# A decoder layer on one core: array quarters in the RWKV products, five last transfers, rows gathered unscaled

## The reference, cut to what matters

```python
def step(state, inp):
    r_t, w_t, k_t, v_t, kk_t, a_t = inp
    sa = jnp.einsum('bhvk,bhk->bhv', state, -kk_t)
    state = (state * w_t[:, :, None, :] + sa[..., None] * (kk_t * a_t)[:, :, None, :]
             + v_t[..., None] * k_t[:, :, None, :])
    return state, jnp.einsum('bhvk,bhk->bhv', state, r_t)
```

```python
h = rms_norm(x, norm_ffn[l])
...
for e in range(N_EXPERTS):
    hid = jax.nn.silu(h @ w_gate[e]) * (h @ w_up[e])
    y = y + combine[..., e:e + 1] * (hid @ w_down[e])
...
return rms_norm(x, norm_final)
```

## Time and profile before

| what | value |
|---|---|
| median of 3 runs | 647.74 us (647.39 to 648.77) |
| the profiled execution | 647.7 us, its span 645.8 us |
| granted PE clock over the span | 0.979 |
| PE busy | 596.3 us (92%) |
| DVE / ACT / POOL busy | 218.3 / 139.2 / 20.6 us |
| DMA | 158.94 MB, mean 246 GB/s |

### The profile page before, as it was taken

One profiled execution on the slowest core, in us unless ns is written; L12 is line 12 of the kernel. 1 busy time (PEld: TensorE's weight loads), 2 busy tenths in 40 slices (PEclk: granted clock), 3 DMA queues, 4 the chain that ended last, 5 costly groups with the idle time before them and its releaser, 6 DMA issues.

```text
span 645.8 us, 11725 instructions
## 1 busy us (share of the span) xinstructions
PE 596.3 (92%) x4936; PEld 434.2 (67%) x4936; DVE 218.3 (34%) x598; ACT 139.2 (22%) x353; POOL 20.6 (3%) x24
## 2 busy tenths in 40 slices
PE   8999999999999999999999999998989988757793
PEld 8988887878877877777788888894434442313241
DVE  3152448625334566356400222234121121102022
ACT  3110233052243353444411000001110111000013
POOL 1000000001100103001000000000000000000000
PEclk9999999999999999999999999999999999969697
DMA  8584344731301111101339993888999999999993
GB/s 320 195 323 176 127 145 160 303 131 66 123 16 62 67 67 67 67 4 66 130 123 420 420 397 137 361 356 312 420 421 421 421 420 420 422 421 421 421 389 108
DMA packets 27287, 158.94 MB, mean 246 GB/s; under 512 B 2896, under 2 KB 7136, under 8 KB 9440
## 3 DMA queue, kind: packets, MB, share of 16 engines
q1 hardware_dynamic: 24224, 137.71, 54.4%
q10 hardware_dynamic: 3008, 20.45, 7.6%
HBM read 157.07 MB, written 1.07 MB: 245 GB/s over the span
## 4 chain that ended last, share of the span: by engine, by line
PE 62%; issue 32%; DVE 3%; ACT 1%; DMA 1%; POOL 0%; POOLq 0%; DVEq 0%; ACTq 0%; SPq 0%
PE bank L615 44%; PE bank L841 3%; PE bank L944 2%; PE bank L647 2%; PE bank L973 2%; PE bank L993 2%; PE bank L630 1%; DMA ring<-front 1%; PE bank L957 1%; ACT tok L1590 1%; PE bank L878 1%; PE bank L897 1%; DVE work L1789 1%; PE bank L908 1%; PE bank L1059 0%
## 5 line engine op out<-in xcount | busy, mean ns | idle before, releaser
L615 PE MATMUL bank<-hT,ring 128*128 128x256 f32 x864 | 199.6, 383 | 0.3 <-ACTq L1433 0.3
L615 PEld LDWEIGHTS bank<-hT,ring 128*128 128x128 f32 x864 | 159.6, 190 | 30.4 <-issue 10.4
L615 PE MATMUL bank<-yT,ring 128*128 128x256 f32 x256 | 55.4, 379 | 0.0
L615 PEld LDWEIGHTS bank<-yT,ring 128*128 128x128 f32 x256 | 48.6, 190 | 6.6
L1421 ACT ACTIVATE work<-bank 128x512 f32<-128x512 f32 (+2 forms) x44 | 22.6, 514 | 107.8 <-PE bank L1240 48.9
L1286 PE MATMUL bank<-ring,work 128*32 128x512 f32 (+1 forms) x192 | 34.7, 649 | 10.6 <-DMA yT<-experts 7.2
L1789 DVE TENSOR_TENSOR work<-bank,table 128x512 f32<-128x512 f32 (+1 forms) x22 | 11.6, 544 | 95.0 <-PE bank L1233 88.3
L1233 PEld LDWEIGHTS bank<-work,tok 128*128 128x128 f32 x256 | 30.2, 192 | 10.0 <-issue 10.0
L1590 ACT ACTIVATE tok<-tok,small 128x128 f32<-128x128 f32 (+1 forms) x64 | 28.4, 445 | 23.0 <-DVE small L2017 21.4
L1233 PE MATMUL bank<-work,tok 128*128 128x128 f32 x256 | 31.5, 278 | 0.8 <-DVE work L1793 0.8
L1224 PE MATMUL bank<-ring,work 128*32 128x512 f32 x240 | 29.6, 597 | 2.9 <-DMA ring<-experts 2.8
(11 more groups left out here) (255 smaller groups left out, 728.4 us busy)
## 6 DMA issues: line engine op xcount, KB each, us to landing
ring<-front SPq DMA_DIRECT2D x47, 1024.0 KB, 4.9
ring<-experts SPq DMA_DIRECT2D x40, 1024.0 KB, 24.6
work<-experts SPq DMA_DIRECT2D x9, 1024.0 KB, 27.7
ring<-experts ACTq DMA_DIRECT2D x8, 1024.0 KB, 13.8
table<-experts SPq DMA_DIRECT2D x6, 1024.0 KB, 27.2
yT<-experts SPq DMA_DIRECT2D x6, 1024.0 KB, 26.8
hT<-experts SPq DMA_DIRECT2D x4, 1024.0 KB, 24.3
work<-experts ACTq DMA_DIRECT2D x3, 1024.0 KB, 28.0
```

The source lines that it names most:

```text
L615: return first(pe.matmul(o, l, r, start=(k == 0), stop=(k == n - 1)))
```

## The change

Four edits.

1. *RWKV products.* For heads of odd `p` (in `solve`: for the second bank) the output's partition half is swapped (`half = c ^ p`), and the loops alternate between the banks, so that neighbours use different quarters. The swap is undone by the copies: DVE's copy of `y{i}1` and ACT's of `xu{i}1` become two copies of 64 partitions each.
2. *Router and seats.* A small table, two memsets and the slot numbers are made ahead of the wait for x. The counting matrix has -1024 on its diagonal, so that a count below zero means membership; `seat` compares the counts in PSUM with shifted slot numbers and writes `sel` itself. `scale_seats` is gone.
3. *Unscaled rows.* The gathered rows lack 1/rms. In each gang PE makes `half_root` for each slot (two matmuls with one column), ACT copies it to SBUF, and it is the scale of the tanh; the square of 1/rms goes into the combine weights. The turned weights of gang 0 come ahead of its last gate and up product.
4. *Last transfers and end.* The last gang's down chunks come in five parts (`PIECES`: each of the two row halves of columns 0 to 511, both halves of 512 to 767, each half of 768 to 1023), 20 transfers. PE works through them as they land. The root is taken by ACT (Sqrt, one token tile after the other) and DVE's reciprocal instead of POOL; DVE copies the second and third part.

```diff
-    put("earlier", (r[:, None] < r[None, :]) * 1.0)
+    put("earlier", (r[:, None] < r[None, :]) * 1.0 - np.eye(P) * OUTSIDE)
...
-                    for n in range(2):
-                        o = begin(f"xu{i}{n}")
-                        for h in range(4):
+                    xbank = [begin(f"xu{i}{n}") for n in range(2)]
+                    for h in range(4):
+                        for n in range(2):
                             for c in range(2):
                                 rows = slice(64 - 64 * c, 128 - 64 * c)
-                                last = pe.matmul(o[64 * c:64 * c + 64, h * P:(h + 1) * P], zinv[rows, 4 * n + h, :],
+                                half = c ^ n
+                                last = pe.matmul(xbank[n][64 * half:64 * half + 64, h * P:(h + 1) * P], zinv[rows, 4 * n + h, :],
                                                  rhs[rows, 4 * n + h, :, :], start=True, stop=True)
...
-                    for p in range(2):
-                        rows = slice(64 * p, 64 * p + 64)
-                        yb = bank[plan[f"y{i}{p}"][0]]
-                        for m in range(4):
-                            last = pe.matmul(yb[64 * c:64 * c + 64, m * DH:(m + 1) * DH],
+                    for m in range(4):
+                        for p in range(2):
+                            rows = slice(64 * p, 64 * p + 64)
+                            last = pe.matmul(y_rows(i, p, c)[:, m * DH:(m + 1) * DH],
                                              ar[rows, m, i, 1, 64 * c:64 * c + 64], state[rows, (2 * i + c) % 2, m, :],
                                              start=False, stop=True, skip_group_check=True)
...
+                    for m in range(4):
+                        for product in range(2):
+                            for p in range(2):
+                                h = 2 * m + p
+                                for c in range(2):
+                                    rows = slice(64 * c, 64 * c + 64)
+                                    right = vrow[rows, h * DH:(h + 1) * DH] if product else rhs[rows, h, 1, :]
+                                    last = pe.matmul(y_rows(i, p, c)[:, m * DH:(m + 1) * DH],
+                                                     amat[rows, h, 1 + 2 * product, :], right,
+                                                     start=(m == product == 0), stop=False, skip_group_check=True)
...
+            def y_rows(i, p, c):
+                half = c ^ p
+                return bank[plan[f"y{i}{p}"][0]][64 * half:64 * half + 64, :]
...
                     for i in range(NT):
+                        pe.matmul(bank[5][:, 0:1], sel[:, i, :], half_root[:, i:i + 1], start=(i == 0), stop=(i == 1))
...
+                        down_part(bank[0], *LAST[0], fs=(0,))
+                        pe.wait_ge(q["late_loaded1"], 16 * GANG)
+                        down_part(bank[0], *LAST[0], fs=(1,))
+                        scatter_last(0, 0)
...
-            pool.wait_ge(q["last_in"], 1)
-            pool.tensor_tensor(stat[:, 8:8 + NT], stat[:, 0:NT], cn("neghalf")[:, 0:NT], ALU.pow).then_inc(q["last_root"], 1)
...
+                            for c in range(2):
+                                ins = copy(rhs[64 * c:64 * c + 64, 4:8, :, :], solved[64 - 64 * c:128 - 64 * c])
...
+            def root(i):
+                act.wait_ge(q["squared"], 2 * NT + i + 1)
+                act.wait_ge(q["last_total"], 1)
+                act.activation(stat[:, i:i + 1], stat[:, 26 + 4 * i:27 + 4 * i], ACT.Sqrt, bias=stat[:, 18 + i:19 + i])\
...
-                    act.activation(gtanh, bank[4][:, 0:DE], ACT.Tanh, scale=0.5).then_inc(q["gtanh_ready"], 1)
+                    act.wait_ge(q["slot_root"], gang + 1)
+                    act.activation(gtanh, bank[4][:, 0:DE], ACT.Tanh, scale=slot_root).then_inc(q["gtanh_ready"], 1)
...
+                    if p == 0:
+                        chain(dve.tensor_copy(yv[:, :, p, :], yb))
+                    else:
+                        for c in range(2):
+                            chain(dve.tensor_copy(yv[64 * c:64 * c + 64, :, p, :], yb[64 - 64 * c:128 - 64 * c]), hold=(c == 1))
...
-            chain(stt(place[:, :, 0:E], b0[:, 0:2 * E].rearrange("p (i e) -> p i e", i=2), 1.0, member, ALU.add, ALU.mult))
...
-                    ts(sel[:, i, :], wsel[:, i, :], stat[:, 8 + i:9 + i], None, ALU.mult).then_inc(q["sel_ready"], 1)
...
+                    o = sel[:, i, :].rearrange("p (e s) -> p e s", e=GANG)
+                    tt(o, like(places[:, i, gang * GANG:(gang + 1) * GANG][:, :, None], [P, GANG, CAP]), slots,
+                       ALU.is_equal).then_inc(q["sel_ready"], 1)
```

More of the change, by code:

```diff
@@ L311, in build_layer @@
         halves = small[:, 192:224]
+        seats = halves
+        half_root, half_square, slot_root = stat[:, 40:42], stat[:, 42:44], stat[:, 44:45]
         rtf = work[:, 8 * S + 2 * E:LOW]
@@ L1281, in gathered_experts, with down_part @@
                     pe.wait_ge(q["ghidT_ready"], gang + 1)
-                    def down_part(n, o, lo, w, release):
-                        for f in range(2):
+                    def down_part(o, lo, w, fs=(0, 1), release=False):
+                        for f in fs:
                             for e in range(GANG):
@@ L1698, in finish @@
                 act.dma_start(out[(NT - 1) * P:NT * P, :], res[:, NT - 1, :]).then_inc(q["stored"], 16)
+            SQUARES = [(n, i) for n in range(len(LAST)) for i in range(NT)]
             def sum_squares(n, i):
@@ L1747, in dense_experts @@
                 second_weight()
-                act.wait_ge(q["root_ready"], 2 * NT + 1)
-                act.wait_ge(q["residual_held"], 2 * NT)
-                for i in range(NT):
-                    copy(tok[:, i, :], tok[:, i, :], scale=stat[:, 8 + i:9 + i]).then_inc(q["xn2_ready"], 1)
                 act.wait_ge(q["wsel_ready"], 1)
@@ L2191, in _ @@
                         chain(tt(merged[:, 2 * n:2 * n + 2, :], macc, mtmp, ALU.add), "merged_ready")
+            fall = cn("falling")
+            pair = [P, EPG, EPG]
+            least = scratch[:, 512:576].rearrange("p (e f) -> p e f", e=EPG)
+            chain(tt(least, like(fall[:, None, 0:EPG], pair), like(fall[:, 0:EPG, None], pair), ALU.is_lt))
+            chain(ts(least, least, 1.2e-38, None, ALU.mult), hold=False)
+            chain(dve.memset(small[:, 112:112 + 2 * (E + GANG)], 0.0), hold=False)
+            chain(ts(seats, fall[:, 0:CAP], -(OUTSIDE + 1.0), None, ALU.add))
             dve.wait_ge(q["x_again"], 16)
@@ L2292, in weigh_seats @@
                     w = wsel[:, i, :].rearrange("p (e s) -> p e s", e=GANG)
-                    ins = tt(w, w, like(combine[:, i, gang * GANG:(gang + 1) * GANG][:, :, None], [P, GANG, CAP]), ALU.mult)
+                    chosen = sel[:, i, :].rearrange("p (e s) -> p e s", e=GANG)
+                    ins = tt(w, chosen, like(combine[:, i, gang * GANG:(gang + 1) * GANG][:, :, None], [P, GANG, CAP]), ALU.mult)
                     if i == 1:
                         ins.then_inc(q["wsel_ready"], 1)
-            seat(0)
-            scale_seats(0)
+            seat(0, counted)
+            chain(dve.tensor_copy(place[:, :, 0:E], counted))
+            dve.sem_inc(bank_free[plan["places"][0]], 1)
+            root = stat[:, 8:8 + NT]
+            chain(ts(half_root, root, 0.5, None, ALU.mult), hold=False)
+            chain(stt(half_square, root, 0.5, root, ALU.mult, ALU.mult), hold=False)
             chain(dve.tensor_reduce(rt("m2"), rt("h2"), AXX, ALU.add))
@@ L2403, in dense_experts @@
                 diagonal_gains()
-                front_gain()
+                for i in range(NT):
+                    front_gain(i)
                 finish()
```

196 lines of the change are left out of this document (85 added, 111 removed).

## The result

The changed kernel takes 643.18 us (median of five runs, 642.21 to 645.20), the kernel before 647.74 (five runs, 647.11 to 648.77). The ratio is 0.9922, 95% interval 0.9906 to 0.9937. Forecast were 642.0 us, within 640.9 to 644.6. The profiled execution of the changed kernel took 642.21 us (span 640.3, and 1.9 around it).

A forecast was written before the change was run, and what follows sets the result against it. PE was taken to bound the first stage, expert transfers the second, a dependent chain the tail. From 647.7 us, less 3.95 (RWKV), 0.2 (gather) and 1.6 (tail), plus 0.1 (transfers), gave 642.0 us, range 640.9 to 644.6.

The forecast's parts named there:

- RWKV: Stage one, where PE sets the time: solve, local y and state y blocks shorten, less 0.4 for copies; 3.95 us gained.
- The waits ahead of the yT turn: Sign: PE's waits between the last y block and the last yT turn grow together by about 0.7 us.
- Rivals 1: RWKV gain is eaten: softmax copies on ACT or longer copies make PE wait; half of 3.95 goes, 644.0 us; chance 0.15.
- rival 5: RWKV y blocks: row halves writing one bank take turns, so they stay as they are; 1.64 us lost, 643.6; chance 0.05.
- rival 2: Front shortens, tail doesn't: last landing or a lagging DMA engine sets the end; 643.7 us; chance 0.13.
- First gather: Router to first gather: DVE ready some 0.8 us sooner, but PE's branch limits the gain; 0.2 us taken.
- Transfers: Expert transfers: same bytes in 20 issues instead of 12; eight more completions in a full queue cost 0.1 us.
- Rival 4: Transfers: issues bind, four more at 1.8 us each are 7.2 us, 649.2 us; chance 0.05.
- Tail: After the last landing: PE's products and scatters end 1.0 us earlier, the root saves 0.55 to 0.65; together 1.6 us.
- The root: End of the tail: ACT root and reciprocal replace POOL's pow, with tile 0 scaled during tile 1's squares; gain 0.55 to 0.65 us.
- Rival 3: Tail: more, shorter waits lower the granted clock from 1.0 to half; +3 us, 645.0 us; chance 0.07.
- The stores: End of the tail: the stores behind the last scaling stay as they are, a change of 0.

The follow-up runs named there:

- y_two_quarters: Changed kernel with both y banks laid out as before, so local y uses two of four quarters, and one copy for each bank: 644.41 us.
- thirtysix_issues: Changed kernel with each transfer of pieces 2 to 5 issued in two halves of 64 partitions, 36 issues instead of 20: 648.38 us.
- combined: Changed kernel with the odd heads' y copies on ACT and both wide tail scatters ahead of the 256-column product: 641.64 us.
- root_on_pool: Changed kernel with the root of the last norm back on POOL, everything else the same: 643.82 us.

## Why the prediction was right, point by point

- **RWKV, 3.95 forecast, 3.90 measured.** The mechanism was right. Solve gave 0.86 twice, as forecast. Local y gave 0.94 instead of 0.82: 64 records over four quarters took 0.98, less than the 1.10 of the earlier trace rows. State y gave 0.28 instead of 0.33. The last of the four was eaten by waits, and the copies lost 0.46 (forecast 0.40). These terms sum to 3.98; where the other 0.08 went I did not trace. The waits ahead of the yT turn grew by 0.46 in all and not by the 0.7 among the signs. Rivals 1 and 5 are out, rival 5 by y_two_quarters too, and rival 2 by the tail below.
- **First gather, 0.2 forecast, 0.31 measured.** The bound by PE's branch was read rightly: the gather now follows it by 0.17 us.
- **Transfers, 0.1 forecast, 0.10 measured.** The agreement to the digit is luck, since the stretch varies by 0.7 between traces; that eight more issues cost next to nothing is what the runs show. Rival 4 was priced wrongly, as a constant for each issue. In thirtysix_issues the issues bind only once SP's lead over the landings is used up; with 20 issues 6 us are left. The larger loss there, fewer bytes at a full share, stood neither in the prediction nor in its rivals.
- **Tail, 1.6 forecast, 1.24 measured.** The step that was mis-sized is "What is left is 1.0 + 0.93 + 0.5 + 0.93 + 0.5 = 3.86". It took 4.33. I had cut shares out of a long row of scatters; alone, a wide scatter takes 1.06 and not 0.93, two narrow ones 1.06, a half product 0.57 to 0.64. What the prediction put at nothing is the change between the two kinds of products. By these rows it costs PE a little over 0.1 us, an estimate: 0.47 over the four changes in this stretch, and 0.27 less in combined, which has two changes fewer (5.12 without its wait, against 1.06 + 4.33). So the PE part gave 0.5 instead of 1.0. The root gave 0.74 instead of 0.55 to 0.65.
- **Rival 3** did not come in the tail: the granted clock is 1.00 in every 2 us window from 616 to 634. The mechanism acted where I had not looked, ahead of the first gather, with a price of 1.5 us.
- **The stores** "stay", I wrote. The last store landed 5.09 us behind its issue in the first trace of before, but 4.30 and 4.31 in the two other traces with its tail, and 5.0 to 5.4 in the eleven traces with the new one or a part of it. Up to 1.0 us of the gain may be lost there. No run tested why; root_on_pool (5.42) speaks against the spacing of the two stores.
- **The number.** The sum of the terms, 5.35, exceeds the 4.56 between the medians. That the profiled 642.21 lies so near to 642.0 is partly luck: the start gave 0.35 that is no part of the change, the tail gave 0.36 less than forecast, and the other four executions are 0.9 to 3.0 us longer. The same two cancel in the last store's issue at 634.62, forecast near 634.6. The 0.8 between 5.35 and 4.56 may be the stores; the spread stays open, as do the runs near 650 us of the kernel before in one set of runs.

## What to carry to other kernels

Price a block by a row of the same shape on the same quarters, and look for who copies its output: crossed halves cost a second copy, which belongs on the engine that is idle just then. Where PE's order is cut finer, count the changes between kinds of products and not only the records. Before a transfer is cut further, read two things: the lead of the last issue over its landing (6.1 us was enough here, 2.4 was not), and the bytes moved at a full DMA share, since pieces of 64 partitions moved 250 GB/s here where those of the changed kernel moved 350 and more.

## What was not expected of the hardware

- The granted clock fell to half at the first gather in two traces, after PE's waits of 1.4 and 0.6 us and of 1.4 and 0.8, and in a third after a wait of 2.45 us. Eight traces with waits of 1.39 and 0.52 us and two with 1.4 and 0.8 kept 1.00. From gather to first issue it cost 1.35 to 1.7 us, and after the longest wait the gather itself came 1.0 us later. A trace that has it can be told by the interval from gather to issue: 3.6 to 4.0 instead of 2.27.
- 64 records of 64x64 over four quarters took 0.98 us in one place and 1.10 in another.
- Splitting a transfer by partitions did not halve what an issue costs SP: 0.60 us for half the partitions, where the changed kernel's last issues took 0.43 to 0.46. And the halves moved 242 to 285 GB/s at a full DMA share, against 350 and more.
